# Norms of the dilated heads' q and k: sums by wide fp32 matmuls, inverse roots on all partitions, in place of per-token columns and a spread back

## The chip, the core and the metric

The kernel runs on one core of one Trainium2 chip. The metric is the device time of one execution in microseconds (us). The engines meant below are TensorE (PE, matmuls into PSUM), VectorE (DVE), ScalarE (ACT) and SyncE (SP, which issues the weight loads). TensorE's granted clock was 1.00 over the whole profiled execution, which is its 2.4 GHz level.

## The reference

Two transformer blocks follow each other on x of 512 tokens x 1024 features. The first has an MLA layer, a sliding-window layer and two MLPs with layer norms. The second, which the change touches, is:

```python
h = rmsnorm(x, g_mix)
z = h @ w_in
zb, zc, zx, zq, zk, zv = split(z, 6 x 512 columns)
y_c = zb * causal_dwconv3(zc * zx, conv_w, conv_b)
q = rmsnorm(zq.reshape(b, t, 8, 64), q_norm_g)      # a norm per token and head
k = rmsnorm(zk.reshape(b, t, 8, 64), k_norm_g)
y_a = dilated_attention(q, k, v)                     # 8 heads, three dilations as one mask
y = concat(rmsnorm(y_c), rmsnorm(y_a));  x = x + y @ w_out
...                                                  # gated feed-forward, then a gated projection
def rmsnorm(a, g):
    return a * rsqrt(mean(a * a, -1) + 1e-6) * g
```

## The kernel before

Activations lie with features on the partitions and the 512 tokens along the free axis, 128 features to a tile. Weights come in 148 slabs of 128 x 2048 fp32, in a fixed order. SyncE loads a slab into one of two stage buffers. ScalarE writes its rounded part w_hi (L437) and VectorE the rest w_lo (L945); both are called `cast` in the code. TensorE multiplies each pair of tiles three times: w_lo with hi, w_hi with hi, w_hi with lo (L1755 to L1757), all 512 tokens wide at a start-to-start distance of 0.23 us, or, in `values`, 256 wide at 0.12 us.

Each engine runs its own list, written out by hand, in order. A list waits for another by semaphore counters. There is no scheduler.

The eight dilated heads are done in two halves of four. Half 0 uses slabs 92 (q), 93 (k), 94 (v) and, for the convolution branch, 95 to 97. Half 1 uses 98 (q), 99 (k), 100 (v) and the slabs of the output projection from 101. A half's q is "q0" or "q1", its k is "k0" or "k1". For each of them the code runs these steps, in this order:

1. TensorE multiplies the slab (`plain`). VectorE multiplies the result by the token norm and so copies it out of PSUM (`qk_out`, L1470), into `tmp[:, 0]` for q and `k_raw`, a part of `d_prob`, for k.
2. ScalarE squares it into `tmp[:, 1]` (L759).
3. TensorE sums the squares of each head (`head_sums`, L2253). The squares are the stationary operand and two columns of the block matrix `ones64` the moving one, so that the sums stand per token on the partitions: 8 matmuls of 2 columns, the result 128 x 16.
4. VectorE scales them (L962), ScalarE takes the root (`root`, L442), VectorE inverts it and does a Newton step (L971 to L974), all on 128 x 16.
5. TensorE spreads the 16 columns back over the head's 64 partitions and 512 tokens (`head_spread`, L2263), 16 matmuls.
6. VectorE multiplies the raw q or k by the gain and the spread factor (`qk_full_out`, L1477). ScalarE writes the rounded part (L774), VectorE the rest (`qk_lo`, L949).

TensorE's list does steps 3 and 5 between the k steps of the next slab's matmuls: for q before step 3 and step 6 of `plain` on the k slab, for k before tiles 1 and 2 of the four token tiles of `values` on the v slab. What follows on TensorE in half 0 is `conv_steps(0)`, the first scores, `conv_steps(1)` and so on. In half 1 it is `mix_tile(0)`, whose fourth k step needs the last tile of `conv_out` (L1443, L945), then the scores, which need `v_out` (L1490) to have read its banks, then `mix_tile(1)`. VectorE takes each convolution tile (`conv_tile`, L1457) and each output tile (`mix_tile`, L1525) from the one PSUM bank 7, so that TensorE can't begin the next before.

The layer norms and the other RMS norms use `root` and `invert_root` too, on 2 or 4 columns.

## Time and profile before

| | us |
|---|---|
| median of 3 runs | 1776.15 |
| lowest, highest | 1775.96, 1777.82 |
| the profiled execution's own time | 1775.99 |
| its span, first to last instruction | 1774.2 |
| TensorE busy | 1753.1 (99%) |
| VectorE busy | 982.9 (55%) |
| ScalarE busy | 670.4 (38%) |

The profile covers one execution. Its own time, 1775.99 us, is 1.8 us above its span and 0.16 us below the median of the runs. A line number is that of the kernel. In a timeline each row gives the start, the duration, the engine, the line and the operation with its output and inputs, and in brackets how long the engine had been idle and whose work ended that. A matmul's modelled duration is longer than its distance to the next one, since matmuls are pipelined. What a piece costs TensorE is read from the starts around it.

### The profile page before, as it was taken

What the parts mean: (1) busy time and instruction counts of PE and PEld (TensorE: products, weight loads), DVE (VectorE), ACT (ScalarE), POOL (GpSimd) and SP (SyncE); (2) the same over time, 40 slices, a digit from 0 to 9 for tenths busy, and PEclk for the clock granted to TensorE, in tenths of its full rate; (3) what the DMA queues carried; (4) which work ended last, traced back from release to release, by engine and by line L of the source; (5) the groups of instructions that cost most, each with busy time, mean ns of one, the idle gap of its engine ahead of it and who ended that gap; (6) DMA issues with size and microseconds to landing.
All of it is one profiled execution on the core that took longest, in us unless ns stands there. A gap on an engine that the chain in (4) does not pass through costs nothing.

```text
span 1774.2 us, 23532 instructions
## 1 busy us (share of the span) xinstructions
PE 1753.1 (99%) x9660; PEld 1501.9 (85%) x9660; DVE 982.9 (55%) x1441; ACT 670.4 (38%) x944; POOL 1.9 (0%) x11
## 2 busy tenths in 40 slices
PE   9999999999999999999999999999999999999999
PEld 7788988888889988998888889888888888888787
DVE  4776752424347576853434247757577665256654
ACT  4555341323233666441313134435355322222332
POOL 0000000000000000000000000000000000000000
PEclk9999999999999999999999999999999999999999
DMA  6223322222222121222222222122222223322341
GB/s 218 96 95 103 112 95 95 95 95 95 95 95 106 62 72 72 86 80 96 95 95 95 95 95 96 72 72 72 72 84 71 95 95 119 119 95 95 119 143 71
DMA packets 28885, 169.74 MB, mean 96 GB/s; under 512 B 2880, under 2 KB 7680, under 8 KB 9728
## 3 DMA queue, kind: packets, MB, share of 16 engines
q1 hardware_dynamic: 22592, 156.44, 24.6%
q10 hardware_dynamic: 6208, 12.08, 2.0%
q8 instruction: 64, 1.05, 0.2%
q14 instruction: 21, 0.17, 0.0%
HBM read 166.39 MB, written 5.27 MB: 97 GB/s over the span
## 4 chain that ended last, share of the span: by engine, by line
PE 91%; DVE 4%; ACT 3%; DMA 1%; issue 1%; SPq 0%; DVEq 0%; ACTq 0%
PE ps L1755 28%; PE ps L1757 28%; PE ps L1756 28%; PE ps L1888 2%; DVE w_lo L945 1%; PE ps L1961 1%; ACT w_hi L437 1%; DMA stage<-slabs 1%; PE ps L1867 1%; PE ps L2131 0%; ACT y L600 0%; PE ps L2263 0%; ACT act_hi L605 0%; PE ps L1828 0%; PE ps L1819 0%
## 5 line engine op out<-in xcount | busy, mean ns | idle before, releaser
L1755 PE MATMUL ps<-act_hi,w_lo 128*128 128x512 f32 (+1 forms) x1512 | 545.8, 361 | 6.3 <-DVE act_lo L945 2.4
L1757 PE MATMUL ps<-act_lo,w_hi 128*128 128x512 f32 (+1 forms) x1512 | 539.2, 357 | 0.0
L1756 PE MATMUL ps<-act_hi,w_hi 128*128 128x512 f32 (+1 forms) x1512 | 538.9, 356 | 0.0
L437 ACT ACTIVATE w_hi<-stage 128x2048 fp32r<-128x2048 f32 (+4 forms) x147 | 268.1, 1824 | 387.1 <-PE ps L1757 385.9
L945 DVE TENSOR_TENSOR w_lo<-stage,w_hi 128x2048 fp32r<-128x2048 f32 (+6 forms) x152 | 323.4, 2129 | 87.9 <-ACT w_hi L437 81.3
L1755 PEld LDWEIGHTS ps<-act_hi,w_lo 128*128 128x128 f32 x1512 | 285.4, 189 | 52.4 <-issue 6.9
L1757 PEld LDWEIGHTS ps<-act_lo,w_hi 128*128 128x128 f32 x1512 | 285.1, 189 | 41.7
L1756 PEld LDWEIGHTS ps<-act_hi,w_hi 128*128 128x128 f32 x1512 | 285.1, 189 | 39.6
L1755 PE MATMUL ps<-hid_hi,w_lo 128*128 128x512 f32 (+1 forms) x608 | 218.4, 359 | 2.1 <-DVE w_lo L945 2.1
L1757 PE MATMUL ps<-hid_lo,w_hi 128*128 128x512 f32 (+1 forms) x608 | 216.9, 357 | 0.0
L1756 PE MATMUL ps<-hid_hi,w_hi 128*128 128x512 f32 (+1 forms) x608 | 215.3, 354 | 0.0
L1755 PEld LDWEIGHTS ps<-hid_hi,w_lo 128*128 128x128 f32 x608 | 114.4, 188 | 18.2 <-issue 2.4
L1757 PEld LDWEIGHTS ps<-hid_lo,w_hi 128*128 128x128 f32 x608 | 114.2, 188 | 18.3
L1756 PEld LDWEIGHTS ps<-hid_hi,w_hi 128*128 128x128 f32 x608 | 114.3, 188 | 17.6
L1172 DVE TENSOR_TENSOR relu<-relu 128x1024 f32<-128x1024 f32 x32 | 39.2, 1225 | 142.0 <-ACT relu L636 136.3
L1052 DVE TENSOR_TENSOR y<-y,ps 128x1024 f32<-128x1024 f32 (+1 forms) x30 | 30.2, 1007 | 111.4 <-PE ps L1757 111.4
L636 ACT ACTIVATE relu<-ps 128x1024 f32<-128x1024 f32 x26 | 26.7, 1027 | 167.0 <-PE ps L1757 167.0
L1755 PE MATMUL ps<-h_hi,w_lo 128*128 128x512 f32 x176 | 69.6, 396 | 2.5 <-DVE w_lo L945 2.0
L1757 PE MATMUL ps<-h_lo,w_hi 128*128 128x512 f32 x176 | 69.0, 392 | 0.0
L1756 PE MATMUL ps<-h_hi,w_hi 128*128 128x512 f32 x176 | 68.3, 388 | 0.0
L1755 PE MATMUL ps<-o_hi,w_lo 128*128 128x256 f32 (+1 forms) x176 | 60.3, 343 | 0.6 <-DVE y L1051 0.6
L945 DVE TENSOR_TENSOR hid_lo<-relu,hid_hi 128x1024 fp32r<-128x1024 f32 x32 | 39.2, 1225 | 36.0 <-ACT hid_hi L639 36.0
(293 smaller groups left out, 2176.2 us busy)
## 6 DMA issues: line engine op xcount, KB each, us to landing
stage<-slabs SPq DMA_DIRECT2D x147, 1024.0 KB, 4.8
bias_rows<-bias_line ACTq DMA_DIRECT2D x1, 3072.0 KB, 13.7
strips<-dilated ACTq DMA_DIRECT2D x2, 1024.0 KB, 4.9
y<-x_t ACTq DMA_DIRECT2D x3, 512.0 KB, 8.9
out<-y ACTq DMA_DIRECT2D x3, 512.0 KB, 2.6
strips<-bias_rows ACTq DMA_DIRECT2D x1, 1024.0 KB, 5.5
strips<-bias_rows ACTq DMA_DIRECT2D x2, 512.0 KB, 4.1
stage<-slabs SPq DMA_DIRECT2D x3, 256.0 KB, 8.3
```

Source lines behind the costliest of these rows:

```text
L437: nc.scalar.activation(w_hi[p][:, 0:w], stage[s][:, 0:w], ACT.Copy).then_inc(cast_hi, 1)
L636: nc.scalar.activation(relu[:, j % 2, :, :], ps[:, b:b + 2, :], ACT.Relu)\
L945: return nc.vector.tensor_tensor(dst, src, f32(hi), ALU.subtract)
L1052: return nc.vector.tensor_tensor(part, part, source, ALU.add)
L1172: nc.vector.tensor_tensor(relu[:, j % 2, :, :], relu[:, j % 2, :, :], relu[:, j % 2, :, :], ALU.mult).then_inc(sqr_done, 1)
L1755: mm(out, l_lo, r_hi, start=start, stop=False, skip_group_check=shared)
L1756: mm(out, l_hi, r_hi, start=False, stop=False, skip_group_check=shared)
L1757: return mm(out, l_hi, r_lo, start=False, stop=stop, skip_group_check=shared)
L1867: last = [nc.tensor.matmul(o, part[l], part[r], start=x == 0, stop=x == 2) for o, part in zip(outs, parts)]
L1888: last = nc.tensor.transpose(ps[:, a.trans_bank + n, c:c + P], prob[:, u % 2, k:k + P], ident)
L1961: last = nc.tensor.matmul(dst, l[rows, tile, q], k[rows, 0:w], start=own and n == 0 and i == group[0], stop=not own and n == 2, skip_group ...
```

## The change

- `head_sums` swaps its operands: `ones64` is stationary and the squares are moving, two fp32 matmuls of 512 columns. The result is the head's mean square on every partition and for every token, 128 x 1024 in two banks. `head_spread` is gone.
- ScalarE takes the inverse root of all 128 x 1024 straight from PSUM (`wide_roots`), with the function Abs_reciprocal_sqrt, into `tmp[:, 1]`. Before it took a root of 128 x 16.
- VectorE does one Newton step on the 128 x 1024 (`wide_step`, three instructions, each waiting for the one before) into `qk_factor`, another part of `d_prob`. It replaces the five instructions on 128 x 16.
- `qk_full_out` reads the factor from SBUF.
- In half 1 VectorE's wait for the third head's transposes (`dil.turned`) stands ahead of the q factors, since these write into `d_prob`.
- All other norms use the same function in `root`, and `invert_root` drops its reciprocal, four instructions to three.
- The engine's function table is loaded for Abs_reciprocal_sqrt where it was for Sqrt. In the built program there are 13 table loads before and 13 now, at the same places.

```diff
@@ -9,6 +9,8 @@
 ACT = mybir.ActivationFunctionType
 F32 = mybir.dt.float32
 F32R = mybir.dt.float32r
+
+RSQRT = ACT.Abs_reciprocal_sqrt
 
 P = 128
 T = 512
...
@@ -47,9 +49,13 @@
 FF_A, FF_B = 12, 10
 
 
+
 NORM = {name: n + 1 for n, name in enumerate(
-    ("mla_q", "mla_kv", "ln0a", "ln0b", "ln1a", "ln1b", "ln2a", "ln2b", "ln3a", "ln3b", "mix", "q0", "k0", "conv", "q1", "k1",
-     "attn", "ffn", "ple"))}
+    ("mla_q", "mla_kv", "ln0a", "ln0b", "ln1a", "ln1b", "ln2a", "ln2b", "ln3a", "ln3b", "mix", "conv", "attn",
+     "ffn", "ple"))}
+
+WIDE = {name: n + 1 for n, name in enumerate(
+    ("q0", "k0", "q1", "k1"))}
 
 SUM_READY = {"mla_q": 1, "mla_kv": 2, "ln": 2, "conv": 19, "ffn": 20, "ple": 21}
 SQUARED = {"mix": 28, "conv": 32, "dil": 33, "ffn": 42, "ple": 46}
...
@@ -246,6 +252,7 @@
         yc, _ = part(KT * T, ("yc", [P, 4, T], F32))
 
         k_raw = d_prob[:, 0, 0:2 * T].rearrange("p (t c) -> p t c", t=2)
+        qk_factor = d_prob[:, 1, 0:2 * T].rearrange("p (t c) -> p t c", t=2)
         h_hi, h_lo, top = part(0, ("h_hi", [P, FF_A, T], F32R), ("h_lo", [P, FF_A, T], F32R))
         gate, gconv, silu, ffh, top = part(
             top, ("gate", [P, 2, T + 2], F32), ("gconv", [P, 2, T], F32), ("silu", [P, 2, T], F32),
...
@@ -439,8 +447,13 @@
             def root(name, width=4, at=0):
 
                 act.wait_ge(var_ready, NORM[name])
-                nc.scalar.activation(tok_s[:, at:at + width], tok_v[:, at:at + width], ACT.Sqrt)\
+                nc.scalar.activation(tok_s[:, at:at + width], tok_v[:, at:at + width], RSQRT)\
                     .then_inc(std_ready, 1)
+
+            def wide_roots(name, dst, sums, scale):
+
+                act.wait_ge(wide_sum, WIDE[name])
+                nc.scalar.activation(dst, sums, RSQRT, scale=float(scale), bias=eps[:, 1:2]).then_inc(wide_root, 1)
 
             def rstd_copy(name, dst, bank):
...
@@ -763,11 +776,11 @@
                 elif half:
                     conv_hi(2)
                 if half and p:
-                    root("k1", 16)
+                    wide_roots("k1", tmp[:, 1, :, :], ps[:, 6:8, :], 1.0)
                     cast(g + p + 2)
                 else:
                     cast(g + p + 2)
-                    root("qk"[p] + str(half), 16)
+                    wide_roots("qk"[p] + str(half), tmp[:, 1, :, :], ps[:, 4 + 2 * p:6 + 2 * p, :], 1.0)
                 if half and p == 0:
                     conv_hi(1)
                 act.wait_ge(qk_full, 2 * half + p + 1)
...
@@ -968,10 +981,16 @@
                 dve.wait_ge(std_ready, NORM[name])
                 if name in ("mix", "attn", "ffn", "ple"):
                     dve.wait_ge(spread_done, NORM[name] - 1)
-                link(nc.vector.reciprocal(r, s))
-                link(nc.vector.scalar_tensor_tensor(q, r, -0.5, r, ALU.mult, ALU.mult))
+                link(nc.vector.scalar_tensor_tensor(q, s, -0.5, s, ALU.mult, ALU.mult))
                 link(nc.vector.tensor_tensor(q, q, v, ALU.mult))
-                nc.vector.scalar_tensor_tensor(r, q, 1.5, r, ALU.add, ALU.mult).then_inc(tok_ready, 1)
+                nc.vector.scalar_tensor_tensor(r, q, 1.5, s, ALU.add, ALU.mult).then_inc(tok_ready, 1)
+
+            def wide_step(name, dst, root, sums, scale):
+
+                dve.wait_ge(wide_root, WIDE[name])
+                link(nc.vector.scalar_tensor_tensor(dst, sums, float(RMS_EPS / scale), root, ALU.add, ALU.mult))
+                link(nc.vector.scalar_tensor_tensor(dst, dst, float(-0.5 * scale), root, ALU.mult, ALU.mult))
+                return nc.vector.scalar_tensor_tensor(dst, dst, 1.5, root, ALU.add, ALU.mult)
 
             def scored_before(a, u, m):
...
@@ -1472,10 +1491,11 @@
 
             def qk_full_out(half, p):
                 raw, gain = ((tmp[:, 0, :, :], "qn_g"), (k_raw, "kn_g"))[p]
+                nc.vector.scalar_tensor_tensor(raw, raw, col(gain), qk_factor, ALU.mult, ALU.mult).then_inc(qk_full, 1)
+
+            def qk_factors(half, p):
                 b = 4 + 2 * p
-                dve.wait_ge(spread_done, NORM["qk"[p] + str(half)])
-                nc.vector.scalar_tensor_tensor(raw, raw, col(gain), ps[:, b:b + 2, :], ALU.mult, ALU.mult)\
-                    .then_inc(qk_full, 1)
+                link(wide_step("qk"[p] + str(half), qk_factor, tmp[:, 1, :, :], ps[:, b:b + 2, :], 1.0))
 
             def qk_lo(half, p):
                 hi, lo, raw, scale = ((dq_hi, dq_lo, tmp[:, 0, :, :], HEAD_SCALE), (dk_hi, dk_lo, k_raw, 1.0))[p]
...
@@ -1529,14 +1549,12 @@
             dve.wait_ge(slab_read, DIL_A)
             qk_out(0, 0)
             cast(DIL_A + 2)
-            mean_squares("q0", 4, 1.0, 16)
-            invert_root("q0", 16)
+            qk_factors(0, 0)
             qk_full_out(0, 0)
             qk_lo(0, 0)
             qk_out(0, 1)
             cast(CONV_B)
-            mean_squares("k0", 6, 1.0, 16)
-            invert_root("k0", 16)
+            qk_factors(0, 1)
             qk_full_out(0, 1)
             qk_lo(0, 1)
             dve.wait_ge(dil_ready, 1)
...
@@ -1582,16 +1600,14 @@
             conv_out(0)
             cast(DIL_B + 2)
             dve.wait_ge(spread_done, NORM["conv"])
-            mean_squares("q1", 4, 1.0, 16)
-            invert_root("q1", 16)
+            dve.wait_ge(dil.turned, 3 * 4)
+            qk_factors(1, 0)
             conv_out(1)
             qk_full_out(1, 0)
             qk_lo(1, 0)
-            dve.wait_ge(dil.turned, 3 * 4)
             qk_out(1, 1)
             conv_out(2)
-            mean_squares("k1", 6, 1.0, 16)
-            invert_root("k1", 16)
+            qk_factors(1, 1)
             cast(MIX_OUT)
             qk_full_out(1, 1)
             qk_lo(1, 1)
...
@@ -2248,22 +2264,8 @@
 
                 pe.wait_ge(qk_sq, n + 1)
                 for k in range(2):
-                    for i in range(4):
-                        c = 8 * k + 2 * i
-                        last = nc.tensor.matmul(ps[:, bank, c:c + 2], tmp[:, 1, k, i * P:(i + 1) * P],
-                                                ones64[:, 0:P:64], start=True, stop=True)
-                last.then_inc(tok_sums, 1)
-
-            def head_spread(name, bank):
-                pe.wait_ge(tok_ready, NORM[name])
-                for k in range(2):
-                    for i in range(4):
-                        for h in range(2):
-                            c, r = 8 * k + 2 * i + h, 64 * h
-                            last = nc.tensor.matmul(ps[r:r + 64, bank + k, i * P:(i + 1) * P],
-                                                    tok_r[:, c:c + 1].broadcast_to([P, 64]), ident,
-                                                    start=True, stop=True)
-                last.then_inc(spread_done, 1)
+                    last = nc.tensor.matmul(ps[:, bank + k, :], ones64, tmp[:, 1, k, :], start=True, stop=True)
+                last.then_inc(wide_sum, 1)
 
             def conv_sums():
                 pe.wait_ge(sum_ready, SUM_READY["conv"])
...
@@ -2325,8 +2327,8 @@
 
             g = DIL_A
             plain(g)
-            plain(g + 1, ready=between({3: lambda: head_sums(0, 4), 6: lambda: head_spread("q0", 4)}))
-            values(g + 2, between({1: lambda: k_sums(0), 2: lambda: head_spread("k0", 6)}))
+            plain(g + 1, ready=between({3: lambda: head_sums(0, 4)}))
+            values(g + 2, between({1: lambda: k_sums(0)}))
             conv_steps(0, range(8))
             pe.wait_ge(slab_read, g + 3)
             pe.wait_ge(dil_ready, 2)
...
@@ -2351,8 +2353,8 @@
             plain(g, ready=between({6: conv_sums}))
             pe.wait_ge(dil.turn_lo, 3 * 4)
             plain(g + 1, ready=between({1: lambda: spread("conv", 7).then_inc(spread_done, 1),
-                                        3: lambda: head_sums(2, 4), 6: lambda: head_spread("q1", 4)}))
-            values(g + 2, between({1: lambda: k_sums(1), 2: lambda: head_spread("k1", 6)}))
+                                        3: lambda: head_sums(2, 4)}))
+            values(g + 2, between({1: lambda: k_sums(1)}))
             mix_tile(0)
             pe.wait_ge(slab_read, g + 3)
             pe.wait_ge(dil_ready, 3 + 2)
```

TensorE's list, during the matmuls of the k slab in half 0, before (mat is `ones64` or the identity):

```order
L1757 MATMUL ps<-act_lo,w_hi 128x512
L2253 MATMUL ps<-mat,tmp 128x2 [waits qk_sq]
L2253 MATMUL ps<-mat,tmp 128x2 x7
L1755 MATMUL ps<-act_hi,w_lo 128x512
L1756 MATMUL ps<-act_hi,w_hi 128x512
...
L1757 MATMUL ps<-act_lo,w_hi 128x512
L2263 MATMUL ps<-mat,tok_r 64x128 [waits tok_ready]
L2263 MATMUL ps<-mat,tok_r 64x128 x15
L1755 MATMUL ps<-act_hi,w_lo 128x512
```

and with the change:

```order
L1773 MATMUL ps<-act_lo,w_hi 128x512
L2267 MATMUL ps<-tmp,mat 128x512 [waits qk_sq]
L2267 MATMUL ps<-tmp,mat 128x512
L1771 MATMUL ps<-act_hi,w_lo 128x512
L1772 MATMUL ps<-act_hi,w_hi 128x512
```

The eight small matmuls are two wide ones, and the sixteen that waited for tok_ready between the same slab's later steps are gone.

VectorE's list in half 1, from the cast of slab 100 to the read of k1, before:

```order
L945 TENSOR_TENSOR w_lo<-stage,w_hi 128x2048 [waits cast_hi]
L962 TENSOR_SCALAR tok_v<-ps 128x16 [waits tok_sums,spread_done]
L971 RECIPROCAL tok_r<-tok_s 128x16 [waits std_ready]
L972 SCALAR_TENSOR_TENSOR tok_q<-tok_r 128x16 [waits dve_link]
L973 TENSOR_TENSOR tok_q<-tok_q,tok_v 128x16 [waits dve_link]
L974 SCALAR_TENSOR_TENSOR tok_r<-tok_q,tok_r 128x16 [waits dve_link]
L1443 SCALAR_TENSOR_TENSOR yc<-yc,vec,rstd 128x512
L945 TENSOR_TENSOR o_lo<-yc,o_hi 128x512 [waits mix_hi]
L1477 SCALAR_TENSOR_TENSOR tmp<-tmp,vec,ps 128x1024 [waits spread_done]
L949 SCALAR_TENSOR_TENSOR dq_lo<-tmp,dq_hi 128x1024 [waits proj_hi]
L1470 TENSOR_TENSOR d_prob<-ps,rstd 128x1024 [waits slab_done,dil_turned]
```

and with the change:

```order
L958 TENSOR_TENSOR w_lo<-stage,w_hi 128x2048 [waits cast_hi]
L991 SCALAR_TENSOR_TENSOR d_prob<-ps,tmp 128x1024 [waits wide_root,dil_turned,spread_done]
L992 SCALAR_TENSOR_TENSOR d_prob<-d_prob,tmp 128x1024 [waits dve_link]
L993 SCALAR_TENSOR_TENSOR d_prob<-d_prob,tmp 128x1024 [waits dve_link]
L1462 SCALAR_TENSOR_TENSOR yc<-yc,vec,rstd 128x512 [waits dve_link]
L958 TENSOR_TENSOR o_lo<-yc,o_hi 128x512 [waits mix_hi]
L1494 SCALAR_TENSOR_TENSOR tmp<-tmp,vec,d_prob 128x1024
L962 SCALAR_TENSOR_TENSOR dq_lo<-tmp,dq_hi 128x1024 [waits proj_hi]
L1489 TENSOR_TENSOR d_prob<-ps,rstd 128x1024 [waits slab_done]
L1462 SCALAR_TENSOR_TENSOR yc<-yc,vec,rstd 128x512
L958 TENSOR_TENSOR o_lo<-yc,o_hi 128x512 [waits mix_hi]
```

Three instructions of 128 x 1024 stand where there were five of 128 x 16, and `conv_out(1)` and `qk_full_out` come behind them. For k1, further down the list, it is the same: the three stand ahead of the cast of slab 101 and of k1's `qk_full_out`.

## Rows read from the trace of the kernel before

**Rows 1.** The page's first part: busy time, share of span, instructions.

```profile
PE 1753.1 (99%) x9660; PEld 1501.9 (85%) x9660; DVE 982.9 (55%) x1441; ACT 670.4 (38%) x944; POOL 1.9 (0%) x11
```

**Rows 2.** Timeline of TensorE, half 0, around q0's sums and spread.

```profile
1154.39 1.84 PE L2253 MATMUL ps<-mat,tmp 128*128 128x2 f32 x16
...
1160.09 0.39 PE L1757 MATMUL ps<-act_lo,w_hi 128*128 128x512 f32 x1
...
1162.64 0.40 PE L1756 MATMUL ps<-act_hi,w_hi 128*128 128x512 f32 x1
```

**Rows 3.** Timeline of TensorE, half 0, around k0's sums and spread.

```profile
1168.33 1.95 PE L2253 MATMUL ps<-mat,tmp 128*128 128x2 f32 x16
...
1172.98 0.28 PE L1757 MATMUL ps<-w_lo,act_hi 128*128 128x256 f32 x1
1173.71 1.97 PE L2263 MATMUL ps<-mat,tok_r 128*64 128x128 f32 x32 [0.45 <-DVE tok_r L974]
...
1175.83 0.28 PE L1756 MATMUL ps<-w_hi,act_hi 128*128 128x256 f32 x1
```

**Rows 4.** Timeline of TensorE: a fp32 matmul of 512 columns (L1934).

```profile
117.86 1.02 PE L1934 MATMUL ps<-rope_raw,mat 128*128 128x512 f32 x2
...
118.95 0.39 PE L1756 MATMUL ps<-c_hi,w_hi 128*128 128x512 f32 x1
```

**Rows 5.** Timeline of VectorE: linked instructions on 512 elements.

```profile
1140.52 0.75 DVE L1422 SCALAR_TENSOR_TENSOR conv<-u_pad,vec,conv 128x512 f32<-128x512 f32 x1
1141.30 0.55 DVE L1418 TENSOR_SCALAR conv<-u_pad,vec 128x512 f32<-128x512 f32 x1
```

**Rows 6.** Timelines of VectorE, ScalarE and TensorE, half 0, in order of time.

```profile
1162.42 1.28 DVE L1477 SCALAR_TENSOR_TENSOR tmp<-tmp,vec,ps 128x1024 f32<-128x1024 f32 x1 [4.12 <-PE ps L2263]
...
1167.22 1.06 ACT L759 ACTIVATE tmp<-d_prob 128x1024 f32<-128x1024 f32 x1 [2.43 <-DVE d_prob L1470]
...
1170.11 2.29 DVE L945 TENSOR_TENSOR w_lo<-stage,w_hi 128x2048 fp32r<-128x2048 f32 x1 [2.92 <-ACT w_hi L437]
...
1175.72 1.28 DVE L1477 SCALAR_TENSOR_TENSOR d_prob<-d_prob,vec,ps 128x1024 f32<-128x1024 f32 x1 [2.07 <-PE ps L2263]
1178.13 1.23 DVE L949 SCALAR_TENSOR_TENSOR dk_lo<-d_prob,dk_hi 128x1024 fp32r<-128x1024 f32 x1 [1.12 <-ACT dk_hi L774]
1181.73 1.23 DVE L1490 TENSOR_TENSOR tmp<-ps,rstd_tok 128x1024 f32<-128x1024 f32 x1 [2.37 <-PE ps L1757]
...
1188.15 0.68 DVE L1457 TENSOR_TENSOR zc<-ps,rstd 128x512 f32<-128x512 f32 x1
...
1189.12 0.50 PE L1755 MATMUL ps<-act_hi,w_lo 128*128 128x512 f32 x1
```

**Rows 7.** Timelines of VectorE and TensorE, half 1, in order of time.

```profile
1254.96 2.29 DVE L945 TENSOR_TENSOR w_lo<-stage,w_hi 128x2048 fp32r<-128x2048 f32 x1 [1.11 <-ACT w_hi L437]
...
1258.43 0.74 DVE L1443 SCALAR_TENSOR_TENSOR yc<-yc,vec,rstd 128x512 f32<-128x512 f32 x1
...
1261.51 1.28 DVE L1477 SCALAR_TENSOR_TENSOR tmp<-tmp,vec,ps 128x1024 f32<-128x1024 f32 x1 [0.95 <-PE ps L2263]
...
1267.52 1.92 PE L2253 MATMUL ps<-mat,tmp 128*128 128x2 f32 x16 [0.24 <-ACT tmp L759]
...
1274.36 1.28 DVE L1477 SCALAR_TENSOR_TENSOR d_prob<-d_prob,vec,ps 128x1024 f32<-128x1024 f32 x1 [0.33 <-PE ps L2263]
...
1280.36 1.23 DVE L1490 TENSOR_TENSOR tmp<-ps,rstd_tok 128x1024 f32<-128x1024 f32 x1 [0.25 <-PE ps L1757]
...
1293.21 0.69 DVE L1525 TENSOR_TENSOR y<-y,ps 128x512 f32<-128x512 f32 x1
...
1294.02 0.48 PE L1755 MATMUL ps<-o_hi,w_lo 128*128 128x512 f32 x1
```

**Rows 8.** Timelines of VectorE and TensorE at the last layer norm, second half.

```profile
1110.56 0.16 DVE L971 RECIPROCAL tok_r<-tok_s 128x2 f32<-128x2 f32 x1
...
1116.89 0.35 PE L1755 MATMUL ps<-act_hi,w_lo 128*128 128x256 f32 x1 [0.41 <-DVE act_lo L949]
```

More of the change, by code:

```diff
@@ L279, in program @@
         norm_z, norm_hi = sem("norm_z"), sem("norm_hi")
+        wide_sum, wide_root = sem("wide_sum"), sem("wide_root")
         c_read, c_full, c_split, c_ready = sem("c_read"), sem("c_full"), sem("c_split"), sem("c_ready")
@@ L581, in layer_norm @@
                     cast(first + 2)
-                load_table(ACT.Sqrt)
+                load_table(RSQRT)
                 if first != SWA_OUT:
@@ L814, in _ @@
             act.dma_start(strips[:, :], dilated[1]).then_inc(strips_landed, 16)
-            load_table(ACT.Sqrt)
+            load_table(RSQRT)
             conv_squares(1)
@@ L898, in _ @@
                         cast(down + j + 2)
-            load_table(ACT.Sqrt)
+            load_table(RSQRT)
             for j in range(8):
```

## The prediction

> **What bounds the kernel now.** I read the page's busy shares first. TensorE is busy 1753.1 of 1774.2 us, the others at most 55% [rows 1], and its clock is granted in full. So a change counts only by what it takes from TensorE's list or adds to it, waits included. VectorE and ScalarE have room on average, but a result that TensorE waits for can still be late. So I then read the timelines of all three engines over the two stretches that the change touches, 1150 to 1190 us and 1250 to 1295 us, and looked for what each piece costs TensorE and who is how early.
>
> TensorE is nearly full there. In half 0 it waits 0.45 us before k0's spread [rows 3]. In half 1 it waits 0.24 us for the squares of k1 [rows 7]. VectorE is the one that waits, 4.12 us for q0's spread, 2.07 us for k0's, 2.37 us for the v slab [rows 6]. That idle time is where the new wide work has to fit.
>
> **What leaves TensorE.** The spread of q0 takes from 1160.09 to 1162.64 with one matmul at 0.23 before and one after it, so 2.55 - 0.46 = 2.09 us [rows 2]. That of k0 takes 1175.83 - 1172.98 - 2 x 0.12 = 2.61 us, its wait among it [rows 3]. The two of half 1 are built the same and I put them at 2.1 each. Together 8.9 us.
>
> **What the sums cost.** The eight narrow matmuls show as one piece of 1.84 to 1.95 us [rows 2, 3, 7]. A fp32 matmul of 512 columns took 118.95 - 117.86 - 0.23 = 0.86 us of TensorE's time [rows 4], so two take 1.72, 1.8 with the drain of the last. I take the sums as ending when they ended before. The bounds are 0.1 us less and 0.1 us more for each of the four.
>
> **What the chain behind them costs.** ScalarE's root over 128 x 1024 is not in the trace. The nearest row is its square on the same size, 1.06 us [rows 6]. I take that. I see no reason for less. The upper bound I set at 1.5, one half more, because neither the function nor its PSUM source is in that row. VectorE's three steps are of the form of `qk_lo`, two tensors and a constant over 128 x 1024, 1.23 us [rows 6]. Linked instructions start their duration plus 0.03 apart (1141.30 - 1140.52 = 0.78 for one of 0.75 [rows 5]). So a step is 1.26 and three are 3.78. Root and steps are 4.9 us with two handovers of 0.03. The upper bound of a step is twice the one on 512 elements, 2 x 0.75 = 1.50 [rows 5]. The lower comes from the instruction with one tensor, which on 512 elements took 0.55 against 0.75 [rows 5], so 1.23 x 0.73 = 0.90.
>
> The first step reads PSUM. `v_out` also reads PSUM, over 128 x 1024, at 1.23 us [rows 7], just what `qk_lo` takes from SBUF [rows 6], so I add nothing. The Trainium skill (VectorE: DVE Perf Modes, the section on the TRN2 errata) gives PSUM sources 120 cycles of fixed cost against 58 for SBUF, at 0.96 GHz. An estimate by that page would add 0.065 us to each of the four first steps, 0.26 in all, and the time would be 1776.1 instead.
>
> **Half 0, walked.** Times are those of the trace before. The sums of q0 end at 1154.39 + 1.84 = 1156.2. The root runs to 1157.3, the steps to 1161.1. VectorE's cast of slab 94 is done by then. So `qk_full_out` starts at 1161.1 instead of 1162.42 [rows 6], 1.3 earlier. From there to the squares of k0 nothing changes (ScalarE's part, `qk_lo`, `qk_out` of k, square). So k0's sums start 1.3 earlier than 1168.33. TensorE could be there 2.1 earlier. Of the 2.1 us of q0's spread it keeps 1.3 and waits for the rest.
>
> The spread of k0 then gives its full 2.6, and TensorE stands 3.9 earlier. VectorE's chain for k0 is later. Its cast, ahead of the steps in its list, ended at 1170.11 + 2.29 = 1172.40 [rows 6], now 1171.1. The root is hidden behind that cast. The steps end at 1174.8, against 1175.72 for the start of `qk_full_out` before, 0.9 earlier. Before, `v_out` waited 2.37 us for TensorE and started at 1181.73. Now VectorE is free for it where `qk_lo` ends, 1178.13 + 1.23 - 0.9 = 1178.4, 3.3 earlier, and the v slab is ready sooner still. Everything behind moves by that, to the first convolution tile, which ended at 1188.15 + 0.68 = 1188.83, 0.29 before TensorE's `conv_steps(1)` at 1189.12 [rows 6]. Handing over takes 0.1 to 0.2 of it. So **half 0 brings -3.4 us**, and the attention loop carries it unchanged, since VectorE and ScalarE run there on TensorE's pace.
>
> **Half 1, walked, without that shift.** Here VectorE had less room. The cast of slab 100 ends at 1257.2 [rows 7], with the root hidden behind it. The steps end at 1261.0. Then comes `conv_out(1)`, with its wait for ScalarE, which took from 1258.43 to 1260.56 (where the 0.95 us of idle time before 1261.51 begin) [rows 7], less 0.1 of overlap. So `qk_full_out` starts at 1263.0, 1.5 **later** than before. The squares of k1 are 1.5 later too, and so k1's sums, at 1269.0 instead of 1267.52. TensorE, 2.1 earlier by q1's spread, waits about 4 us there.
>
> The sums end at 1270.85, the root at 1271.9, the steps at 1275.75, and the cast of slab 101, which stands behind them now, at 1277.95. `qk_full_out` starts there instead of at 1274.36 [rows 7], 3.6 later. `conv_out(3)` is 3.6 later. TensorE reaches `mix_tile(0)` about when qk_full comes, runs three k steps and waits for the fourth, some 2.2 us. `v_out`, which had waited 0.25 [rows 7], is 3.3 later, and so are the first bias and output tiles, all on VectorE's list without a gap to take it up. The last of them that counts is the third output tile, which ended at 1293.21 + 0.69 = 1293.90, directly before TensorE's next tile at 1294.02 [rows 7]. So **half 1 costs +3.3 us**. Behind it VectorE waits for TensorE again, and nothing grows.
>
> **The other norms.** A reciprocal of 0.16 us and its link leave each. It only counts where TensorE waits for the normed tiles. That is at the last layer norm, 0.41 us at 1116.89 with a chain through 1110.56 [rows 8]. I take -0.2 us. The mla, conv, ffn and ple norms hide behind matmuls.
>
> **The sum.** -3.4 + 3.3 - 0.2 = -0.3 us. The profiled execution took 1775.99, so 1775.7, and the median of the runs is 0.16 above it: **1775.8 us**. TensorE loses 8.9 us of work and gets about as much in new waits. The step's price counts nearly in full in all four blocks, twelve steps in all. The root counts in two of them, q0 and k1.
>
> **The rivals.** A measurement of this kernel can tell about 0.2% from no change, 3.6 us.
>
> (a) The steps are short. If an instruction with a constant and two tensors ran as the one-tensor form does, 0.90, the end would move by 12 x 0.33 = 4.0 us, to 1771.9. Against it speaks each two-tensor row of 128 x 1024, 1.23 to 1.28 [rows 6, 7]. 11%. The Trainium skill (VectorE: DVE Perf Modes, The perf-mode tier table) lets fp32 instructions with two tensors run only at one element a cycle, so by that page this rival falls. The rows agree.
>
> (b) The waits that I find aren't there and TensorE keeps its whole gain, because a step that I place on the chain isn't needed where I put it. Then 1776.15 - 8.9 - 0.2 = 1767.1. The 0.24 us wait for k1's squares and the 0.45 before the spread [rows 3, 7] speak against it: the chain is already as late as TensorE. 6%.
>
> (c) Slower. VectorE's list in half 1 is the bound, and a step over 128 x 1024 that reads and writes the same tile costs 1.50, the root 1.5. Then 12 x 0.27 + 2 x 0.44 = 4.1 us are added, 1779.9. It decides at 0.32 us more per step than I take, (3.6 + 0.3) / 12. For it speaks that no row shows this function, against it that such steps on 512 elements took the ordinary 0.75 [rows 5]. 13%.
>
> (d) The change loads tables more often, because the new function shares no set with the square or the copy. The built program has 13 loads as before, so this has no chance of its own.
>
> **How the numbers follow.** The forecast has 70% and lies within 0.2%. Faster are (a) and (b), 17%. Slower is (c), 13%. The range reaches to (a) at 1771.9 and to (c) at 1779.8. What lies outside is (b) and about half of (c), some 13%, with a little of the tails.
>
> **What would show it.** TensorE's busy time is 8 to 9 us lower and its span is not. L2263 is gone. The two wide sums take 1.7 to 1.8 us. TensorE waits about 1.2 us for ScalarE's square before k0's sums, about 4 us before k1's, about 2 us inside `mix_tile(0)`, and under 1 us each before the next scores and `mix_tile(1)`. VectorE is busy 10 to 12 us longer. `conv_steps(0)` starts 3.9 us earlier, half 1 starts 3.4 earlier, and the fourth output tile at the same time as before. I am wrong if the steps are not 1.2 to 1.3 us long, if the wait before k1's sums is under 2 us, or if half 1 costs less than half 0 brings by over 1 us.

## The result and the profile after

| | before | after |
|---|---|---|
| median, 20 runs each | 1777.48 | 1781.14 |
| lowest, highest | 1775.61, 1779.59 | 1778.60, 1786.29 |
| the profiled execution | 1775.99 | 1782.07 |
| its span | 1774.2 | 1780.3 |
| mean granted clock over the profiled execution | 1.000 | 0.995 |

The ratio is 1.0022, with a 95% interval from 1.0015 to 1.0028. The changed kernel is slower by about 3.7 us and lies above the forecast range. The kernel before came out at 1777.48 over 20 runs, 1.3 us above the three runs that the forecast started from. So a part of the distance to the forecast is this starting point, and the +3.7 us is the change's own.

The page's first part of the kernel after, to be held against [rows 1]:

```profile
PE 1753.1 (98%) x9484; PEld 1496.4 (84%) x9484; DVE 991.3 (56%) x1418; ACT 674.4 (38%) x944; POOL 1.9 (0%) x11
```

TensorE has 176 matmuls fewer and is exactly as long busy as before. So some of the matmuls that are left must take longer than they did. The stretch view of TensorE, half 1 of the kernel after, shows why. Its columns are the stretch in us, its length, TensorE's busy time with the number of matmuls, the granted clock (1.00 is 2.4 GHz, 0.50 is 1.2 GHz), the DMA share and GB/s:

```profile
1262.00:1266.00 4.00, 1.13 (x10) 1.00 0.00 0
1266.00:1268.00 2.00, 0.91 (x1) 0.70 0.00 0
1268.00:1270.00 2.00, 2.00 (x5) 0.50 0.00 0
1270.00:1272.00 2.00, 2.00 (x15) 0.95 0.00 0
1272.00:1282.00 10.00, 9.46 (x70) 1.00 0.28 102
1282.00:1284.00 2.00, 0.44 (x2) 0.97 0.04 16
1284.00:1288.00 4.00, 4.00 (x14) 0.50 0.00 0
1288.00:1292.00 4.00, 4.00 (x10) 0.50 0.00 0
1292.00:1294.00 2.00, 2.00 (x6) 0.50 0.04 8
1294.00:1296.00 2.00, 2.00 (x13) 0.97 0.00 0
```

The clock falls twice, once near the end of a wait of TensorE and once right behind one. The timeline of TensorE, same kernel and place (start, duration, and in brackets the wait with its releaser):

```profile
1267.09 3.50 PE L2267 MATMUL ps<-tmp,mat 128*128 128x512 f32 x4 [3.97 <-ACT tmp L772]
...
1283.56 0.56 PE L1771 MATMUL ps<-o_hi,w_lo 128*128 128x512 f32 x1 [2.10 <-DVE o_lo L958]
...
1289.32 0.63 PE L1772 MATMUL ps<-o_hi,w_hi 128*128 128x512 f32 x1
1289.74 0.63 PE L1773 MATMUL ps<-o_lo,w_hi 128*128 128x512 f32 x1
```

These are the two waits that were forecast, about 4 us before k1's sums and about 2 us inside `mix_tile(0)`. Behind the second the matmuls of 512 columns stand 0.42 us apart instead of 0.23, for some 10 us. The Trainium skill (TensorE: Matmul & The Clock Gate, Wait — 56ns, not 53.3ns?) gives 426.7 ns for that distance at the lower clock, and the trace agrees.

There is a third such stretch in this execution, ahead of the changed code, behind a wait of 1.82 us that both kernels have at 1139 us. The stretch view, first of before, then of after:

```profile
1140.00:1144.00 4.00, 4.00 (x20) 1.00 0.00 0
```

```profile
1140.00:1144.00 4.00, 4.00 (x12) 0.57 0.00 0
```

To see what each part costs I take the time between three landmarks, VectorE's reads of the q slab of half 0, the q slab of half 1 and the fourth output tile. They are, of before and of after, in VectorE's timelines:

```profile
1150.60 1.23 DVE L1470 TENSOR_TENSOR tmp<-ps,rstd 128x1024 f32<-128x1024 f32 x1 [0.58 <-PE ps L1757]
...
1248.74 1.23 DVE L1470 TENSOR_TENSOR tmp<-ps,rstd 128x1024 f32<-128x1024 f32 x1 [1.74 <-PE ps L1757]
...
1297.08 0.68 DVE L1525 TENSOR_TENSOR y<-y,ps 128x512 f32<-128x512 f32 x1
```

```profile
1152.17 1.23 DVE L1489 TENSOR_TENSOR tmp<-ps,rstd 128x1024 f32<-128x1024 f32 x1 [2.17 <-PE ps L1773]
...
1246.82 1.23 DVE L1489 TENSOR_TENSOR tmp<-ps,rstd 128x1024 f32<-128x1024 f32 x1 [1.95 <-PE ps L1773]
...
1303.16 0.69 DVE L1545 TENSOR_TENSOR y<-y,ps 128x512 f32<-128x512 f32 x1 [0.24 <-PE ps L1773]
```

| profiled execution | up to the first | half 0 | half 1 | rest |
|---|---|---|---|---|
| before | 1150.60 | 98.14 | 48.34 | 477.1 |
| after | 1152.17 (+1.57) | 94.65 (-3.49) | 56.34 (+8.00) | 477.1 (0) |

Half 0 did what the forecast said (-3.4). Half 1 did not (+3.3 forecast, +8.0 measured).

### The profile page after: what moved, and what is told of

Its sections match the earlier page's. It is cut to its first block, busy times and chain, and to the rows that moved or that the text cites. A ratio compares the mean times of both kernels' runs of the same rounds, so it can differ in the third digit from the quotient of the medians.

```text
span 1780.3 us, 23157 instructions
## 1 busy us (share of the span) xinstructions
PE 1753.1 (98%) x9484; PEld 1496.4 (84%) x9484; DVE 991.3 (56%) x1418; ACT 674.4 (38%) x944; POOL 1.9 (0%) x11
## 4 chain that ended last, share of the span: by engine, by line
PE 89%; DVE 5%; ACT 3%; DMA 1%; issue 1%; SPq 0%; DVEq 0%; ACTq 0%
PE ps L1771 28%; PE ps L1773 28%; PE ps L1772 27%; PE ps L1904 2%; DVE w_lo L958 2%; PE ps L1977 1%; ACT w_hi L445 1%; DMA stage<-slabs 1%; PE ps L1883 1%; PE ps L2147 0%; ACT y L613 0%; PE ps L2267 0%; ACT act_hi L618 0%; PE ps L1835 0%; PE ps L2054 0%
## 5 line engine op out<-in xcount | busy, mean ns | idle before, releaser
L1773 PE MATMUL ps<-o_lo,w_hi 128*128 128x256 f32 (+1 forms) x176 | 59.4, 338 | 0.0
```

What stands on the lines that cost most here:

```text
L1773: return mm(out, l_hi, r_lo, start=False, stop=stop, skip_group_check=shared)
```

## The experiments

Theory A is that the clock takes the difference: the new waits drop TensorE to its lower level, and the matmuls behind them run at half speed. The rivals are B, that VectorE's list in half 1 is longer than I walked and the clock doesn't matter, C, that the 1.57 us lost ahead of half 0 belongs to the change, and D, that the second low stretch is only a tail of the first. All ratios are to the kernel before, with 95% intervals.

**e1, TensorE kept busy through the two waits.**

```diff
+            def fill(n):
+                for i in range(n):
+                    nc.tensor.matmul(ps[:, 6, :], w_hi[place(DIL_A)][:, 0:P], act_hi[:, i % KT, :],
+                                     start=True, stop=True)
...
             def k_sums(half):
...
+                fill((0, 15)[half])
                 head_sums(2 * half + 1, 6)
...
             def mix_tile(j):
...
                     if j == 0:
+                        if k == 3:
+                            fill(8)
                         pe.wait_ge(act_ready, MIX_Y + 2 + k + 1)
```

> The changed kernel with filler: 15 fp32r matmuls of 512 columns (about 3.5 us at 0.23 each) stand ahead of TensorE's wait for the squares of k1, and 8 (1.8 us) ahead of the wait for the fourth convolution tile in mix_tile(0). They write bank 6, which nobody needs then, and add no result. Theory A, the clock: the two new waits of 4.0 and 2.1 us drop TensorE to its 1.2 GHz level and that costs what was not forecast. With TensorE busy through them the granted clock stays 1.00 from 1264 to 1296 us, the tiles of mix_tile(1) stand 0.23 apart, and the ratio to before is 1.000 (0.999 to 1.001), 3 to 4 us under the changed kernel's 1.0022. Theory B, lateness: VectorE's list in half 1 is simply longer than I walked, and the clock only stretches matmuls that would have waited anyway. Then the fourth output tile is as late as with the change and the ratio stays 1.002.

Measured: 1.0009 (1.0000 to 1.0018). That is in A's range and outside B's 1.002. But the median is only 1.6 us below the changed kernel's (1779.54 against 1781.14), where 3 to 4 us were expected. TensorE's timeline and stretch view in half 1 (L2272 is the filler):

```profile
1267.70 1.97 PE L2272 MATMUL ps<-act_hi,w_hi 128*128 128x512 f32 x8
1270.12 1.98 PE L2267 MATMUL ps<-tmp,mat 128*128 128x512 f32 x4 [0.45 <-ACT tmp L772]
...
1289.48 0.39 PE L1772 MATMUL ps<-o_hi,w_hi 128*128 128x512 f32 x1
1289.71 0.40 PE L1773 MATMUL ps<-o_lo,w_hi 128*128 128x512 f32 x1
```

```profile
1268.00:1270.00 2.00, 1.67 (x8) 1.00 0.00 0
1270.00:1272.00 2.00, 1.88 (x5) 1.00 0.00 0
...
1284.00:1288.00 4.00, 3.54 (x19) 1.00 0.02 4
1288.00:1292.00 4.00, 3.21 (x14) 1.00 0.00 0
```

The clock is whole, the distance is 0.23 again. From VectorE's reads half 0 takes 94.67 us and half 1 51.69, which is 3.35 more than before, against 8.00 with bare waits. So in half 1 of the profiled executions the clock took 4.65 us, and what is left is the forecast's +3.3. B falls. As a whole this execution gains less, since it ran 10 us at the lower clock elsewhere, behind a wait of 0.58 us that before has too (0.59, with the clock at 1.00 behind it):

```profile
77.48 0.33 PE L1977 MATMUL ps<-kn_hi,act_lo 128*128 128x128 f32 x1 [0.58 <-DVE negmax L1011]
```

```profile
78.00:88.00 10.00, 10.00 (x38) 0.52 0.01 2
```

The first landmark stands at 1155.27. With the other norms changed and no low stretch ahead of it, it stands at 1150.37 (e2 below), so this stretch cost 4.90 us. The span less this, 1778.5 - 4.9 = 1773.6, is 0.6 under before's 1774.2.

The other runs of e1 fit that. Six of the eleven stand at 1779.5 to 1780.3 with a mean clock of 0.997, as the profiled one. The other five are at 1776.6 to 1778.7 with 0.998 or 0.999. None of the 26 runs of before in the same comparison is below 0.998. So the trace shows what the filler gives back in half 1, and by their mean clock most runs of e1 lose several us again. That they lose them where the profiled one does, no trace shows, and why e1 loses them so much more often than before is open.

**e2, e3, e4: one part alone.** In e2 half 1 has its narrow sums and spreads back, in e3 half 0, in e4 both, so that only the other norms are changed. The core of e2:

```diff
+            mean_squares("q1", 4, 1.0, 16)
+            invert_root("q1", 16)
+            conv_out(1)
+            qk_full_old(1, 0)
+            qk_lo(1, 0)
             dve.wait_ge(dil.turned, 3 * 4)
-            qk_factors(1, 0)
-            conv_out(1)
-            qk_full_out(1, 0)
-            qk_lo(1, 0)
             qk_out(1, 1)
...
-                                        3: lambda: head_sums(2, 4)}))
-            values(g + 2, between({1: lambda: k_sums(1)}))
+                                        3: lambda: head_sums_old(2, 4), 6: lambda: head_spread("q1", 4)}))
+            values(g + 2, between({1: lambda: k_sums(1), 2: lambda: head_spread("k1", 6)}))
```

> The change in half 0 (q0, k0) and in the other norms, half 1 built as before, with narrow sums and spread. My walk of half 0 gives -3.4 us, the other norms -0.2, together -3.6: ratio 0.998. Theory A (clock): no new wait over 1.6 us is left, so it should come out as walked, 0.998. Theory C, that the +1.6 us that the changed kernel has already lost when it comes to q0's sums (1155.96 against 1154.39 us) belongs to the change: then -2.0 us, 0.999.

> The change in half 1 (q1, k1) and in the other norms, half 0 built as before. By the walk alone it is +3.3 - 0.2 = +3.1 us, ratio 1.0017. Theory A (clock): the two new waits are there and both are followed by a stretch at half clock, +3.1 and 4 to 6 us more, ratio 1.004 to 1.005. Theory B (no cost of the clock, VectorE's list only): 1.0017 plus whatever the list is longer than I walked, but with the granted clock's drop making no difference, which run e1 tells.

> The kernel before with the change in the norm function alone: Abs_reciprocal_sqrt in place of Sqrt, the reciprocal gone, the dilated heads' norms on 16 columns as before. The walk gives -0.2 us, ratio 0.9999. Theory C, that the new function or its handling is what made the changed kernel 1.6 us late before half 0: +1.4, ratio 1.0008. Theory A says of that 1.6 us that it is a half-clock stretch after a wait that both kernels have (1139 us, 1.82 us long) and that falls in some executions of either kernel: then the ratio is 1.000 and single runs of both kernels differ by such steps.

| | median | ratio | first landmark | half 0 | half 1 |
|---|---|---|---|---|---|
| e2, half 0 wide | 1773.65 | 0.9980 (0.9970 to 0.9989) | 1150.37 | 94.64 | 48.33 |
| e3, half 1 wide | 1784.17 | 1.0038 (1.0024 to 1.0052) | 1151.94 | 97.87 | 55.48 |
| e4, norms only | 1777.08 | 0.9999 (0.9990 to 1.0008) | 1152.10 | 97.82 | 48.32 |

e2 comes out as walked. It is faster than before and than the changed kernel, and it does the whole computation. e3 costs more than the walk's 1.0017 and slightly less than A's 1.004. Its half 1 is 7.1 us longer, with waits of 4.0 and 1.3 us. The clock falls to 0.50 in the first and 2.6 us behind the second. Its first landmark is 1.57 us later than e2's, behind a stretch of 3.4 us at 0.50 from 77.7 us on. C falls by e2, whose ratio excludes C's 0.999 and whose first landmark is 0.23 us earlier than before's, with the new function in it. e4's median alone wouldn't decide it, as C's 1.0008 is the end of its interval. Its profiled execution has the low stretch at 1140 us, e2's hasn't, and their first landmarks differ by 1.73 us. The other norms bring 0.23 us up to half 0 (1150.60 to 1150.37). In e3 and e4 the old half 0 is 0.3 shorter too. That fits k0's spread, which had waited 0.45 us for the narrow chain [rows 3] that lost its reciprocal here.

The medians can be added up without any trace. Against before's 1777.37, e2 is 3.72 us faster, e3 6.80 slower, and e4, which is contained in both, 0.29 faster. Together this is +3.4, against +3.7 for the whole change. So over whole runs, too, half 1 costs more than walked: e3's 6.80 us are 3.7 above the walk's +3.1.

**e5, e6: one wait filled.** As e1, with `fill((0, 15)[half])` alone in e5, and `fill(8)` alone in e6.

> The changed kernel with the 15 filler matmuls ahead of the wait for the squares of k1 only. Theory A (clock): no stretch at half clock behind that wait, 1.4 us back. The second wait (2.1 us, in mix_tile(0)) is left bare, and the 10 us at half clock behind it stay: the granted clock reads 0.50 about 1284 to 1294 us, half 1 (from the read of q1's slab to the fourth output tile) is 3.3 us longer than before with the clock whole and stays at 6 to 8 us longer here. Theory D, that the second stretch is only the long tail of the first wait: with that one filled it goes too, and half 1 is 3.3 us longer.

> The changed kernel with the 8 filler matmuls in mix_tile(0) only, the 4.0 us wait before k1's sums bare. Theory A (clock, each wait by itself): about 3 us at half clock behind the first wait as with the change, none behind the second, half 1 about 3.3 + 0 to 1.4 = 3.3 to 4.7 us longer than before. Theory D: the second stretch comes though its wait is filled, half 1 is 7 to 8 us longer.

Measured: 1.0009 (1.0000 to 1.0018) and 1.0005 (0.9996 to 1.0014). Half 1 is 53.19 and 53.55 us long, 4.9 and 5.2 more than before. TensorE's stretch view, e5 (first wait filled), then e6 (second filled):

```profile
1270.00:1282.00 12.00, 9.88 (x72) 1.00 0.24 87
1282.00:1284.00 2.00, 2.00 (x8) 0.56 0.00 0
1284.00:1288.00 4.00, 4.00 (x12) 0.50 0.01 4
```

```profile
1264.00:1266.00 2.00, 0.47 (x1) 0.65 0.00 0
1266.00:1270.00 4.00, 4.00 (x9) 0.50 0.00 0
...
1280.00:1300.00 20.00, 19.32 (x96) 1.00 0.19 72
```

The bare wait has its low stretch, the filled one has none, and neither needs the other. D falls. In e5 half 1 came out shorter than A's 6 to 8 us, because the stretch was 7 us long and not 10. In e6 it came out longer than A's 3.3 to 4.7, as the stretch at the first wait was 7 us long here and 3.4 in after. Above the 3.35 us of the walk, one bare wait costs 1.5 and 1.9 us. With both bare it was 4.65, as the second stretch was 10 us long there and 7 in e5. These are single executions. The medians of e1, e5 and e6, 1779.54, 1778.95 and 1778.63, don't separate one filled wait from two.

**e7, e8: the wait of both kernels at 1139 us filled**, in e2's kernel and in the kernel before.

```diff
             g = DIL_A
+            for i in range(7):
+                nc.tensor.matmul(ps[:, 7, :], w_hi[place(g - 1)][:, 0:P], act_hi[:, 0, :], start=True, stop=True)
             plain(g)
```

> The change in half 0 alone (as e2, ratio 0.998), and 7 filler matmuls of 512 columns (1.6 us) into the free bank 7 ahead of the first slab of half 0, where both kernels wait 1.82 us at 1139 us. Theory A (clock): no execution loses the 1.6 us there, the runs stand at e2's lower group, 1772.0 to 1772.5 us, median 1772.2, ratio 0.9970 to 0.9975. Without theory A it is e2 again, 1773.7, or worse by what the filler adds.

> The kernel before with the same 7 filler matmuls and nothing else changed. Theory A (clock): the executions of before that take about 1777.5 us at a mean clock of 0.999 are those in which the 1.82 us wait at 1139 us is followed by a stretch at half clock; with the wait filled all but a few stand at 1775.7 to 1776.2, ratio 0.999 to 0.9995. If the two groups have another cause, both stay, ratio 1.000.

Measured: e7 median 1773.46, 0.9976 (0.9965 to 0.9986), e8 median 1777.30, 0.9994 (0.9985 to 1.0003). Both expectations missed. The 30 runs of before in this comparison fall in groups by their mean clock: 7 at 1775.8 to 1776.4 (1.000), 17 at 1777.3 to 1777.7 (0.999), 6 above. With the wait filled both groups are still there (e8: four runs at 1775.9 to 1776.1, seven above). So the stretch at this wait isn't the only thing that makes the second group, or the filler doesn't keep it away in every execution. The profiled executions of e7 and e8 both are of the lower group, at 1.00, and can't tell. Stretches outside the changed code stand in other traces at 77 us (e1, e3, e5), 1278 us (e11) and 1677 us (e6). Filling one place brought nothing clear of the noise. What makes the second group is open.

**e9 to e11: a pause of a set length in the kernel before**, where nothing but TensorE sets the pace. The cut shows e10 with its 6 writes, e9 has 3 and e11 has 11.

```diff
+            pool.wait_ge(halt, 1)
+            for i in range(6):
+                if i:
+                    pool.wait_ge(resume, i)
+                nc.gpsimd.memset(idle[:, :], 0.0).then_inc(resume, 1)
...
+            def pause(k):
+                if k == 4:
+                    latest[-1].then_inc(halt, 1)
+                    pe.wait_ge(resume, 6)
...
-                ups(first + 24)
+                for j in range(4):
+                    plain(first + 24 + j, ready=pause if (first, j) == (MLP1, 1) else None)
```

> The kernel before with one pause of TensorE of about 1 us, in the middle of slab 82 (second MLP, plain matmuls, where TensorE alone sets the pace): TensorE signals GpSimd, which writes an unused tile three times, and TensorE waits for that. Theory L: a pause costs its own length, about +1 us, ratio 1.0006, the granted clock behind it 1.00. Theory A (clock): the pause may drop TensorE to its 1.2 GHz level for some us, each of which costs half of itself. In the traces so far waits of 0.6 us were followed by such a stretch in some executions, so I expect +1 to +3 us.

> The same with a pause of about 2 us (six writes). Theory L: +2 us, ratio 1.0011. Theory A: behind the 2.1 us wait in mix_tile(0) 7 to 10 us ran at half clock, which would cost 3.5 to 5 us more: +5.5 to 7 us, ratio 1.003 to 1.004. Behind the 1.8 us wait at 1139 us there was such a stretch in only two of the eight profiles that have that wait bare, so it may also fall in some executions only, and the single times then stand in groups.

> The same with a pause of about 4 us (eleven writes). Theory L: +4 us, ratio 1.0023. Theory A: the 4.0 us wait before k1's sums was followed by a stretch at half clock in all three profiles that had it bare, 3 to 7 us of it while TensorE worked: +5.5 to +7.5 us, ratio 1.003 to 1.004.

The matmul behind the pause, of e9, e10 and e11 in turn, and then the stretch behind it of e10 and e11:

```profile
1023.19 0.50 PE L1762 MATMUL ps<-act_hi,w_lo 128*128 128x512 f32 x1 [1.16 <-POOL idle L417]
```

```profile
1024.30 0.80 PE L1762 MATMUL ps<-act_hi,w_lo 128*128 128x512 f32 x1 [2.27 <-POOL idle L417]
```

```profile
1026.23 0.80 PE L1762 MATMUL ps<-act_hi,w_lo 128*128 128x512 f32 x1 [4.11 <-POOL idle L417]
```

```profile
1024.00:1028.00 4.00, 3.70 (x9) 0.57 0.70 207
1028.00:1032.00 4.00, 4.00 (x19) 1.00 0.14 59
```

```profile
1028.00:1032.00 4.00, 4.00 (x11) 0.50 0.16 64
1032.00:1036.00 4.00, 4.00 (x19) 0.97 0.00 0
```

The last column but one is how much later TensorE starts the last layer norm's first tile (1116.89 in before [rows 8]), with no other low stretch in between:

| | wait | median | ratio | later at 1116.89 | beyond the wait |
|---|---|---|---|---|---|
| e9 | 1.16 | 1778.96 | 1.0008 (0.9999 to 1.0017) | 1.40 | 0.2 |
| e10 | 2.27 | 1781.86 | 1.0025 (1.0016 to 1.0035) | 4.08 | 1.8 |
| e11 | 4.11 | 1784.70 | 1.0043 (1.0029 to 1.0056) | 7.24 | 3.1 |

Theory L falls for 2 and 4 us, as both intervals lie above its 1.0011 and 1.0023. In e9 the clock stayed at 1.00, and 0.2 us came on top of the wait even so. e9 and e11 came out in their forecast ranges. The forecast of e10 (5.5 to 7) was too high, as I had taken the stretch behind `mix_tile(0)` for the rule. The medians bear the column out over 5 to 11 runs each: 1.6, 4.5 and 7.4 us above before's 1777.33.

**e12, the three steps left out** (ScalarE's root is used unrefined in all four blocks, so part of the computation is missing):

```diff
-                link(nc.vector.scalar_tensor_tensor(dst, sums, float(RMS_EPS / scale), root, ALU.add, ALU.mult))
-                link(nc.vector.scalar_tensor_tensor(dst, dst, float(-0.5 * scale), root, ALU.mult, ALU.mult))
-                return nc.vector.scalar_tensor_tensor(dst, dst, 1.5, root, ALU.add, ALU.mult)
```

> The changed kernel without VectorE's three steps in all four blocks (ScalarE's inverse root is used as it is, so the Newton refinement of the heads' factor is left out). My walk says that each step counts nearly in full: without the 3.78 us per block the chain is ahead of TensorE in every block, the waits of 1.2, 4.0 and 2.1 us are gone or under 1 us, and TensorE keeps the 8.9 us of the spreads but for the wait for squares right behind the sums of q. With theory A there is then no loss of clock either: 1768 to 1770 us, ratio 0.9945 to 0.996. If something other than the chain of steps held half 1 back, the ratio would stay above 0.998.

Measured: 1769.63, 0.9959 (0.9945 to 0.9972). Half 0 takes 92.84 us (-5.3) and half 1 46.08 (-2.3), and no wait of TensorE there is over 0.8 us. So 7.6 of the 8.9 us stay once the steps are gone. It is the steps that turn them into waits.

## Why the prediction was wrong

**The steps that held.** The two wide sums of q0 take TensorE 1.72 us, from 1155.96 to 1157.91 less one matmul of 0.23, as forecast:

```profile
1155.96 1.88 PE L2267 MATMUL ps<-tmp,mat 128*128 128x512 f32 x4
...
1157.91 0.39 PE L1772 MATMUL ps<-act_hi,w_hi 128*128 128x512 f32 x1
```

VectorE's steps are 1.22 to 1.23 us long and start 1.26 apart, the root takes 1.12 against the 1.06 taken. VectorE's timeline of the kernel after, half 0:

```profile
1159.02 1.23 DVE L991 SCALAR_TENSOR_TENSOR d_prob<-ps,tmp 128x1024 f32<-128x1024 f32 x1 [0.41 <-ACT tmp L456]
1160.28 1.23 DVE L992 SCALAR_TENSOR_TENSOR d_prob<-d_prob,tmp 128x1024 f32<-128x1024 f32 x1
1161.54 1.22 DVE L993 SCALAR_TENSOR_TENSOR d_prob<-d_prob,tmp 128x1024 f32<-128x1024 f32 x1
1162.80 1.28 DVE L1494 SCALAR_TENSOR_TENSOR tmp<-tmp,vec,d_prob 128x1024 f32<-128x1024 f32 x1
```

The first step, which reads PSUM, is no longer than the others, 1.23 and 1.23. The estimate by the Trainium skill (VectorE: DVE Perf Modes, the section on the TRN2 errata), 0.065 us more for it, isn't seen. The walk of half 0 gave -3.4, measured -3.49. Its path holds too. TensorE's `conv_steps(1)` waits for VectorE's first convolution tile, 3.49 us earlier than before once the 1.57 us ahead of half 0 are taken off (1189.12 [rows 6] + 1.57 - 1187.20):

```profile
1187.20 0.50 PE L1771 MATMUL ps<-act_hi,w_lo 128*128 128x512 f32 x1 [0.30 <-DVE zc L1476]
```

The walk of half 1 gave +3.3, measured +3.35 with the clock held (e1). The other norms were put at -0.2, measured -0.23. Up to half 0 and through both halves this makes -0.4 us against the forecast's -0.3. The waits, forecast at 1.2, 4 and 2 us, are in the trace after at 1.2 (5.2 less 4.0), 4.0 and 2.1. The columns are the us waited in total, the number of waits and the longest:

```profile
PE ps L2267 <- ACT tmp L772: 5.2, 2, 4.0
PE ps L1771 <- DVE o_lo L958: 2.1, 1, 2.1
```

VectorE's extra busy time was put too high at 10 to 12 us. It is 991.3 - 982.9 = 8.4: 14.7 us of wide steps came, and 6.3 left, 3.5 of them reciprocals and 2.8 the other steps on 16 columns. The ends of the range don't quite match their terms. (a) gives 1771.8 and (c) 1779.9, where the range says 1771.9 and 1779.8.

**The step that failed** is the term "half 1 costs +3.3 us". It measured +8.00. The walk priced each new wait of TensorE at its own length, and the prediction's opening, that the clock "is granted in full", left the sum without a term for what a wait does to the clock. At two of the new waits the granted clock fell to 0.50, and the matmuls behind them stood about twice as far apart. With both waits filled half 1 cost 3.35 (e1), so the missing term is 4.65 us in the profiled execution of after. The further 1.8 us at 1140 us (1.57 + 0.23) isn't the change's. Of the 12 profiles that have the wait there bare, five show the stretch (after, e4, e9, e10, e12), and e4, e9 and e10 have the old halves.

So the profiled span is -0.4 + 4.65 + 1.8 = +6.1, as measured (1780.3 - 1774.2). In the medians it is +3.7. Before's profiled execution stands 1.5 us under its median and after's 0.9 over its own, and 6.1 - 1.5 - 0.9 = 3.7. Most runs of before lose some time to the clock too: in the comparisons that list it, those at 1775.7 to 1776.4 have a mean clock of 1.000, the others 0.999 or less.

The starting point was off as well. Counted from before's 1777.48 the range would end at 1781.1, where the measured median lies. That would have been luck, since the range had room there for longer steps (c) and not for the clock.

**The signs the forecast named.** It said TensorE's busy time would fall by 8 to 9 us. It didn't, and that is the reading that points to the clock. The fourth output tile was to start at the same time as before and starts 6.1 us later. "Half 1 costs less than half 0 brings by over 1 us" was named as a refutation only in one direction. The other came: half 1 cost 8.0 and half 0 brought 3.5.

**The rivals.** (a) and (b) did not happen. (c) named the right place, half 1, and came near with 1779.9, but that is luck: its cause was longer steps, and they took 1.23, not 1.50, the root 1.12, not 1.5. A rival with the clock was missing. [Rows 7] could have carried it, with 4 us of idle TensorE worked out while TensorE's longest wait in the middle of before is 1.8 us. The forecast should have said that what such a wait costs beyond its length is unknown, and left room for it on the slower side.

**Why the whole gain was lost.** The change takes 8.9 us from the fullest engine and puts 14.7 us of wide steps on the next one in the chain. In half 0 VectorE had waited for TensorE 4.12, 2.07 and 2.37 us at these places [rows 6], and 3.5 us stayed. In half 1 it had waited 0.95, 0.33 and 0.25 [rows 7], and there the change is worth undoing: e2, which keeps the wide form in half 0 only, is 0.9980 (0.9970 to 0.9989) of before.

## What to carry to other kernels

Price an idle gap of TensorE at its own length only if it is short. In a dense stretch of this kernel 1.2 us cost 1.4, 2.3 us cost 4.1 and 4.1 us cost 7.2. When a change takes work from TensorE, walk the chain behind it for each place by itself, and keep it only where the next engine waits for TensorE. If TensorE's busy time doesn't fall though matmuls were removed, read the granted clock by short stretches first.

## What the runs showed of the hardware

- TensorE's granted clock fell to 0.50 at waits in the middle of dense matmuls, and stayed there for 3 to 10 us, most of it with matmuls one behind the other. At a wait of about 4 us that came in the profiles of all four kernels that had one bare (after, e3, e6, e11), and began 0.3 to 1.2 us before the wait's end. Behind 2.1 and 2.3 us it came in all three (after, e5, e10).
- Low stretches stand behind shorter waits too, in some executions: behind 0.6 us at 77 us in e1 (10 us), e3 and e5 (3.4 us each) and in none of the other eleven profiles, and behind 1.3 us at 1677 us in e6 alone. That these waits are their cause is not shown. Once, in e11 at 1278 us, it fell with no wait over 0.24 us in the 18 us before it.
- What a low stretch costs is about half of it, as far as TensorE sets the pace: the 10 us at 0.52 made the landmark behind it 4.90 us late. The Trainium skill (TensorE: Matmul & The Clock Gate, Terms) gives the same rule, the throttled time times one minus the share of the clock. In half 1, where VectorE sets the pace in part, it costs less: the 7 us stretch of e5 cost 1.5 us, and TensorE's wait of 0.79 us for VectorE at that place in e1 is gone in e5.
- 15 and 8 useless matmuls in the waits kept the clock at 1.00. They wrote a free PSUM bank and read operands that lay in SBUF.
- ScalarE's Abs_reciprocal_sqrt over 128 x 1024 from PSUM took 1.12 us, Square from SBUF 1.06.
